# One of four weight sums of a Strassen chunk, made by VectorE and not by an adding transfer

## The reference, cut to what matters

```python
def swiglu(h, w_gate, w_up, w_down):
    return (jax.nn.silu(h @ w_gate) * (h @ w_up)) @ w_down

for i in range(DEPTH):                      # DEPTH = 2
    ...
    h = h + y                               # y: conv module or attention
    h = h + swiglu(rmsnorm(h, ffn_norm_g[i]), ffn_w_gate[i], ffn_w_up[i], ffn_w_down[i])
return rmsnorm(h, final_norm_g)
```

## Time and profile before

| | us |
|---|---|
| median of three runs | 1991.01 |
| lowest, highest | 1988.06, 1994.06 |
| the profiled execution, its own time | 1993.24 |
| its span, first to last instruction | 1991.4 |

### The profile page before, as it was taken

How to read it: one execution, slowest core, us unless ns; L and a number is a source line. 1 busy time by engine, 2 the same in 40 slices (tenths; PEclk the granted TensorE clock), 3 DMA queues, 4 the chain that set the end, 5 groups by cost and what they waited for, 6 DMA issues and landing times.

```text
span 1991.4 us, 25065 instructions
## 1 busy us (share of the span) xinstructions
PE 1955.9 (98%) x9934; PEld 1671.0 (84%) x9934; DVE 1614.3 (81%) x1769; ACT 1141.2 (57%) x1138; POOL 227.7 (11%) x196
## 2 busy tenths in 40 slices
PE   8999899999999999999999999999999999999998
PEld 7999888888888888888888998888888888888886
DVE  6999886888888888888876775588888888888885
ACT  5898744555556555555544654355555555555553
POOL 0555400010011000110010000000010000101002
PEclk9999999999999999999999999999999999999999
DMA  8999464899998999889845444559989999999983
GB/s 272 257 259 236 148 214 148 240 271 278 254 235 241 261 279 262 223 242 263 258 145 151 123 143 174 190 174 287 243 216 273 259 279 239 236 253 262 277 211 127
DMA packets 253830, 453.37 MB, mean 228 GB/s; under 512 B 18708, under 2 KB 60444, under 8 KB 251420
## 3 DMA queue, kind: packets, MB, share of 16 engines
q1 hardware_dynamic: 207968, 349.73, 50.5%
q0 software_dynamic: 44256, 98.57, 28.8%
q10 hardware_dynamic: 1500, 3.61, 0.5%
HBM read 435.10 MB, written 2.10 MB: 220 GB/s over the span
## 4 chain that ended last, share of the span: by engine, by line
PE 87%; DMA 7%; DVE 3%; ACT 1%; issue 1%; SPq 0%; POOL 0%; ACTq 0%; DVEq 0%; POOLq 0%
PE ps L1802 83%; DMA raw<-in_conv_w_pw_dram 4%; DMA w_lo<-raw 3%; DVE ps L1311 1%; PE ps L2043 1%; ACT w_lo L772 1%; PE ps L2297 0%; PE ps L2298 0%; PE ps L2278 0%; DMA resid<-in_x_dram 0%; DVE w_lo L1188 0%; PE ps L1833 0%; SPq L557 0%; PE ps L1852 0%; PE ps L1841 0%
## 5 line engine op out<-in xcount | busy, mean ns | idle before, releaser
L1193 DVE TENSOR_TENSOR w_lo<-raw,w_hi 128x2048 fp32r<-128x2048 f32 x224 | 509.2, 2290 | 148.3 <-ACT w_hi L927 148.0
L927 ACT ACTIVATE w_hi<-raw 128x2048 fp32r<-128x2048 f32 x224 | 426.3, 1916 | 347.7 <-PE ps L1802 209.1
L1802 PE MATMUL ps<-w_hi,x_hi 128*128 128x512 f32 x1168 | 456.0, 390 | 0.9 <-DVE x_lo L1220 0.9
L1802 PE MATMUL ps<-w_hi,x_lo 128*128 128x512 f32 x1168 | 454.9, 389 | 0.0
L1802 PE MATMUL ps<-w_lo,x_hi 128*128 128x512 f32 x1168 | 454.8, 389 | 0.0
L1802 PE MATMUL ps<-w_hi,a_hi 128*128 128x512 f32 (+1 forms) x768 | 292.7, 381 | 0.0
L1802 PE MATMUL ps<-w_hi,a_lo 128*128 128x512 f32 (+1 forms) x768 | 292.3, 381 | 0.0
L1802 PE MATMUL ps<-w_lo,a_hi 128*128 128x512 f32 (+1 forms) x768 | 292.2, 380 | 0.0
L1802 PEld LDWEIGHTS ps<-w_hi,x_hi 128*128 128x128 f32 x1168 | 219.3, 188 | 47.1 <-DVE x_lo L1220 1.4
L1802 PEld LDWEIGHTS ps<-w_hi,x_lo 128*128 128x128 f32 x1168 | 219.3, 188 | 45.7
L1802 PEld LDWEIGHTS ps<-w_lo,x_hi 128*128 128x128 f32 x1168 | 219.3, 188 | 45.2
(11 more groups left out here) (242 smaller groups left out, 2992.7 us busy)
## 6 DMA issues: line engine op xcount, KB each, us to landing
raw<-in_ffn_w_down_dram SPq DMA_DIRECT2D x66, 1024.0 KB, 8.3
raw<-in_ffn_w_up_dram POOLq DMA_DIRECT2D x60, 1024.0 KB, 8.8
raw<-in_ffn_w_gate_dram SPq DMA_DIRECT2D x50, 1024.0 KB, 6.6
raw<-in_ffn_w_up_dram SPq DMA_DIRECT2D x48, 1024.0 KB, 6.4
row_bc<-in_ffn_w_gate_dram SPq DMA_DIRECT2D x38, 1024.0 KB, 5.9
raw<-in_conv_w_pw_dram SPq DMA_DIRECT2D x64, 512.0 KB
row_bc<-in_ffn_w_down_dram SPq DMA_DIRECT2D x22, 1024.0 KB, 5.8
b<-in_ffn_w_up_dram SPq DMA_DIRECT2D x40, 512.0 KB, 5.8
```

The source lines that it names most:

```text
L927: act.activation(f_w_tile(w_hi, l, q), f_raw_tile(l, q), ACT.Copy).then_inc(f_hi_done, 1)
L1193: dve.tensor_tensor(f_w_tile(w_lo, l, q), f_raw_tile(l, q), hi32(f_w_tile(w_hi, l, q)), ALU.subtract).then_inc(f_lo_done, 1)
L1802: ins = pe.matmul(dst, lhsT, rhs, start=first and n == 0, stop=last and n == len(pairs) - 1, skip_group_check=skip)
```

## The change

T2, the weights of Q6, is made on VectorE: `t2_sum` adds Q3's raw tile (buffer 1) to T1 (buffer 0) in place. ScalarE's `q6_hi` waits for that sum (`t2_sum_done`), not for a transfer. GpSimd no longer issues Q6's adding transfer. Q7's adding transfer overwrites buffer 1, which the sum reads, so it now waits for the sum, and not for Q3's low part.

```diff
@@ weight_sums, GpSimd
                 def add(c, p):
                     q = f_pos(c, p)
-                    wait_f_lo(pool, l, f_before(q, f_raw))
+                    if p == Q7:
+                        pool.wait_ge(t2_sum_done, chunk_no(l, c) + 1)
+                    else:
+                        wait_f_lo(pool, l, f_before(q, f_raw))
                     pool.dma_start(f_raw_tile(l, q).rearrange("p (k n) -> p k n", k=GK), w_of(l, p, c),
                                    accum_op=ALU.add).then_inc(f_added[f_raw(q)], 16)
                 for c in range(1, FC):
-                    for p in (Q5, Q7, Q6, Q4):
+                    for p in (Q5, Q7, Q4):
                         add(c, p)
@@ ffn, ScalarE
+                def q6_hi(c):
+                    act.wait_ge(t2_sum_done, chunk_no(l, c) + 1)
+                    f_hi(l, f_pos(c, Q6))
...
-                    parts_hi(c, D1, Q6)
+                    parts_hi(c, D1)
+                    q6_hi(c)
@@ ffn, VectorE
+                def t2_sum(c):
+
+                    x, q = f_raw_tile(l, f_pos(c, Q5)), f_pos(c, Q5)
+                    wait_f_lo(dve, l, q)
+                    dve.tensor_tensor(x, x, f_raw_tile(l, f_pos(c, Q3)), ALU.add).then_inc(t2_sum_done, 1)
...
                     t2_lo_and_t4(c)
+                    t2_sum(c)
                     parts_lo(c, D1, Q6)
```

More of the change, by code:

```diff
@@ L158, in f_sum @@
 def f_sum(q):
-    return F_FIRST <= q < F_LAST and f_part(q) in (Q5, Q6, Q4, Q7)
+    return F_FIRST <= q < F_LAST and f_part(q) in (Q5, Q4, Q7)
 def ring_slot(l, slot):
@@ L168, in f_loads @@
 def f_loads(q):
-    return not (F_FIRST <= q < F_LAST and f_part(q) in (R2, R3, R4))
+    return not (F_FIRST <= q < F_LAST and f_part(q) in (Q6, R2, R3, R4))
 F_RAW_SLOTS = RING + 1
@@ L398, in encoder @@
         t_sum = sem("t_sum")
+        t2_sum_done = sem("t2_sum_done")
         t1_hi_done = sem("t1_hi_done")
@@ L920, in f_hi @@
                 landed = 16 * (F_LAYER[f_raw(q), f_sum(q)] * l + F_LOADED[q])
-                act.wait_ge(f_added[f_raw(q)] if f_sum(q) else f_in[f_raw(q)], landed)
+                if f_loads(q):
+                    act.wait_ge(f_added[f_raw(q)] if f_sum(q) else f_in[f_raw(q)], landed)
                 before = f_before(q, f_w)
```

## The result

| | us |
|---|---|
| before, median of five runs (lowest to highest) | 1991.01 (1988.06 to 1994.06) |
| after, median of five runs (lowest to highest) | 2064.75 (2059.45 to 2067.79) |
| ratio, 95% interval | 1.0368 (1.035 to 1.0386) |
| profiled execution after: its own time, its span | 2064.75, 2062.9 |

The change costs 73.7 us, not 27.

A forecast was written before the change was run, and what follows sets the result against it. TensorE's unbroken matmuls were taken to bound the kernel. Sixteen middle chunks (15.2 us), two first (9.0) and two last (2.8) made 27 us, put on the 1991.0 median: 2018 us, 1.4% slower, range 2001 to 2036.

The forecast's parts named there:

- the mechanism named: Q7's adding transfer, issued only after the sum, makes VectorE's mix late; TensorE stops 0.83 us at Q7 in middle chunks.
- The transfer is not hidden: Denies a rival: Q7's transfer lands in under 8.27 us, middle chunks lose nothing; 1997 us with 7.5; chance 0.12.
- That is nearest to Q4's case ...; I take 9.2.: Q7's transfer in a middle chunk: 9.2 us from issue to landing, as Q4's 9.3 has a load of D3 beside it.
- the rival of the longer transfer: Q7's transfer takes 9.7 to 11.2 us beside Q2's load, D2's tail and Q4's transfer; 2028 to 2058 us, chance 0.18.
- Q2's high part ... is done at 467.0 and just not late.: On ScalarE behind Q7's high part in a middle chunk: Q2's high part was to delay nothing on the way to the mix.
- 9.03 was forecast: Middle chunk: from Q7's landing through ScalarE's and VectorE's steps to the end of the mix, 9.03 us.
- 24.5 forecast (the 27 without the restarts): TensorE's waits alone: at Q7 0.83 us in middle chunks, 2.5 in first, 1.3 in last; at D1 1.8 in first.
- No term for the granted clock: The prediction took the granted clock as 1.00 in both profiled stretches and counted no loss from it.
- The restart at 0.1: TensorE's first matmul after a stop takes 0.50 and not 0.39 us, so a 0.83 us stop was counted as 0.95.
- D1's term in first chunks: First chunk of each layer: the sum delays D1's low part, so TensorE starts D1 1.8 us late, 1.9 with restart.

The follow-up runs named there:

- experiment 1: Changed kernel, but the sum adds T1 to itself and Q7's adding transfer again waits only for Q3's low part: 1995.42 us, ratio 1.002 to the kernel before.
- experiment 3: Changed kernel without the load of Q2, whose product is made of what lies in the buffer: 2020.16 us, ratio 1.0135 to the kernel before.
- experiment 5: Changed kernel with the sum directly behind Q5's low part and the hidden activations' low part ahead of the first half-size sum: 1996.67 us, ratio 1.0024.
- experiment 6: Changed kernel without Q2's load, and with the mix ahead of the second down group and Q2's low part: 2003.78 us, ratio 1.0064.
- experiment 2: Kernel before, no sum, Q6's transfer kept; Q7's adding transfer issued behind Q6's and waiting for D1's low part: 2091.44 us, ratio 1.0487.
- experiment 7: Changed kernel with the sum behind D1's low part, so Q2's load is issued earlier and Q7's transfer later: 2070.66 us, ratio 1.0422.

## Why the prediction was right or wrong

**Right.** Slower, by the mechanism named. The sum takes 2.28 us, GpSimd's issue follows 0.30 behind it (0.29 forecast), Q6's removed transfer gives nothing back, the sums by themselves cost next to nothing in middle chunks (experiment 1), and TensorE waits at Q7 in every chunk and at D1 in the first ones. The transfer is not hidden. The rule of the Trainium skill, "DMA: Bandwidth & Descriptors", section "Anatomy of one DMA — SWDGE (gpsimd) path", which gave 4.4 us as an estimate for 1 MiB, agrees with no run: issue to landing of all such transfers after (least, median, most) is

```profile
DMA to landing us min/median/max: 8.4/9.9/15.6
```

**Wrong in size.** Four steps of the sum failed:

- *"That is nearest to Q4's case ...; I take 9.2."* The twenty Q7 transfers took 9.4 to 10.6, some 9.9 on average. 0.7 us in each of twenty chunks is 14 us. The nearer row was Q6's 10.1, taken with another transfer under way; I gave it to the rival of the longer transfer, whose range of 2028 to 2058 is nearer but ends short as well. Without Q2's load the transfer took 8.6 (experiment 3).
- *"Q2's high part ... is done at 467.0 and just not late."* It is late. The way from landing to mix is 10.05 us in the chunk shown (603.21 to 613.26), where 9.03 was forecast; 0.99 of the excess is VectorE's wait for Q2's high part. By the forecast's own times VectorE wants that part at 468.5, so it had 1.5 us in hand, and the load, issued at 455.9, could take 10.6 us. At its old 5.4 the step held with room; at 12.17 it failed. I had priced what that load does to the transfer, and not what the transfer does to the load. Over all chunks that is some 10 us: waits of 48.9, less 24.5 forecast (the 27 without the restarts), less 14.
- *No term for the granted clock.* I took it as 1.00 throughout, since a stretch before had it so. The chunk whose wait was 2.80 us ran at 0.95 and lost 5.9. In all it is some 16 us.
- *The restart at 0.1.* A wait costs its gap and 0.29 more, by the chunk of 64.49; 0.2 in 22 waits are some 4 us.

27 + 14 + 10 + 16 + 4 = 71 us, against 71.5 measured. The 14 is from twenty transfers; the 10 and the 16 are what is left when other terms are taken off, so the split between them is no better than a few microseconds.

D1's term in first chunks was too high, 1.3 each for 1.8; the 0.5 us each are within the 4.

Without Q2's load the change costs 29 us (experiment 3), close to the 27 forecast. That is in part luck: the waits there are 18.6 us (15.6 at the mix, 3.0 at D1), where 24.5 were forecast, and the sum had no term for what stands around them.

**Still open.** The clock fell behind seven of twenty waits. It follows the waits (experiments 1, 5 and 6, which have few or none in the FFN, show no fall there), but what picks the seven was not tested: they are 2.06 to 5.31 us long, and waits of 2.28 and 2.90 us had no fall behind them. Q2's load took 12.17 us where it was issued behind Q7's transfer, and 5.6 and 5.2 where it was issued ahead of one (experiments 2 and 7). So its time goes by the order of issue; why was not tested, nor what Q4's transfer, which also runs beside the load, adds to it. The queues in the next section fit it.

## What to carry to other kernels

When an edit moves a transfer, list what else is issued within its flight time, and price both: what the neighbour does to it and what it does to the neighbour. A path that has 0.8 us too little, twenty times, is not a loss of twenty times 0.8, since every step that was "just not late" behind it becomes late too, and the clock may fall behind the waits. Place a new instruction where a late transfer's issue keeps its old slack: the same sum, four entries earlier in VectorE's list (and the low part of the hidden activations one earlier), cost 5 us in place of 74.

## What the runs showed of the hardware

The queues in the stretch from 593 to 604 us of the changed kernel (packets, MB, share of sixteen engines' time):

```profile
q0 software_dynamic: 558, 1.11, 57.2%
q1 hardware_dynamic: 429, 0.88, 22.3%
```

GpSimd's adding transfers (Q7's and the start of Q4's) took 57.2% of the transfer engines' time for 1.11 MB, SP's loads 22.3% for 0.88 MB: twice as much engine time for each MB (0.515 to 0.253 of the stretch). Over the whole run before it is the same, 28.8% for 98.57 MB against 50.5% for 349.73. I had not expected an adding transfer to take more than a load of its size does. GpSimd's queue holds nothing but adding transfers here, so whether the adding or the queue is the reason is not shown.

The times to landing of the chunks shown go by the order of issue. Q7's transfer takes 8.6 us with no load of Q2 beside it, 9.6 with the load issued 1.9 us behind it, 11.5 with the load 0.26 us ahead and 8.8 with it 2.5 us ahead. The load takes 5.4 us before, 12.17 behind the late transfer, 5.6 and 5.2 ahead of it. In these chunks the one issued first keeps its time, or loses a microsecond; the other pays 2.9 and 6.8 us where 0.26 and 1.9 us lie between the issues, and 0.2 where 2.5 do.

The granted clock falls to its lower level behind waits of a few microseconds that come once in a chunk of 62 us, though not behind all, and such a fall can cost as much as the wait it followed (in the chunk shown 2.8 us, 5.9 less the wait of 2.80 and some 0.3 around it).
